# Attention heads taken in pairs in a one-core trunk-layer kernel: unpadded keys, normalised probabilities, transposed output

## The chip, the cores and the metric

One core of one Trainium2 chip runs the kernel. The metric is the device time of one execution in microseconds. The profile is one more execution of the same program.

## The reference, cut to what matters

One trunk layer (adaLN, softmax attention beside a gated linear attention, two branch projections merged by gates, an output projection, a mixture of 32 experts) in float32 for 256 latent and 128 context tokens of width 1024. The part that the change touches:

```python
# 8 query heads, 2 key/value heads, head_dim 64
if latent:
    keys = concat([axial_rope(k_a), ctx_k]); vals = concat([v_a, ctx_v])   # 256 + 128 keys
else:
    keys, vals = k_a, v_a                                                  # 128 keys
sc = einsum('bqkgd,btkd->bkgqt', qblk, kf) * scale
p = softmax(sc, axis=-1)
attn = einsum('bkgqt,btkd->bqkgd', p, vf)
merged = gates[:, :, 0] * (attn @ w_br_attn) + gates[:, :, 1] * (gla @ w_br_gla)
```

## The kernel before, in words

The 384 tokens are three tiles of 128 (0 and 1 latent, 2 context). Engines run programs of their own and meet at semaphores. TensorE's program is written out by hand: it runs 27 projections (`PROJ`, L105; L1478: 8 matmuls of 128x512, each recorded as two MATMULs, as every float32 matmul that is not a transpose), and after projection `j` it works off the list `AFTER[j]` (L108 to L146), which holds small steps of the two attentions. VectorE, ScalarE and GpSimd walk the same lists in the same order (VectorE through `STEPS`, L147). So the small steps of TensorE come between two projections, and VectorE's and ScalarE's part of them runs beside the next projection.

Softmax attention is 24 head jobs (`HEAD_JOBS`, L106: tile 2, then 0, then 1; eight heads each). Two of them go through per step `m`, which lies behind projection `15 + m` (the last three steps, 11 to 13, all lie behind projection 26). In a step TensorE first transposes the probabilities of the two heads of the step before (`pT`, L1615: three 128x128 transposes per latent head, one per context head), then makes the scores of two new heads (`score`, L1608), then multiplies the two heads of two steps before with the values (`pv`, L1626). In the steps 1, 4 and 7 the four transposes of a finished tile of the linear attention (`gT`, L1531) come first.

A score takes all 128 rows: `qT` holds a head of each key/value half in its two row halves (rows 0 to 63 and 64 to 127), and `kTl`, `kTc` hold the keys of each half with zeros in the other 64 rows. VectorE copies them there (L943, two copies per tile) and GpSimd sets the zeros at the start (L620). `score` on VectorE is the negated maximum (L971); ScalarE takes the exponential with its row sum (L1316) into one of four buffers `Pr`. VectorE copies the transposes into `PTr` (L981). `pv` has the transposed probabilities as the stationary operand (128 columns) and 64 columns of the values as the moving one, into `outb[tile]`, tokens in the partitions. When a tile's eight heads are through, VectorE divides by the row sums (`aout`, L986 and L987). Behind all steps TensorE transposes the three tiles (`aT`, L1531), ScalarE copies them to `attnT` (L1332), and the branch projections begin (L1650).

What sets the order around the change: the side jobs (`pT`, `score`, `gT`, `kT`, `z` and others) take three PSUM banks in turn (`Banks`, L150; `side_jobs`, L188), and `claim` waits until the bank's last reader is through. In a step of two `pT` and two `score` jobs the second score has the bank of the first `pT`, which VectorE must have copied out (L981). `gout3` on VectorE (L961 to L964, in the steps 0, 3 and 6) stands behind the step's `score` entry and gives the `gated` that `gT` waits for one step on. The sync queue loads `w_br_attn` and `w_br_gla` (L542) once their weight buffer is free, and `w_out` and the first experts when `aT` of tile 1 is copied (L554).

```python
for _m in range(len(HEAD_JOBS) // 2 + LAG):
    _j = min(15 + _m, len(PROJ) - 1)
    for _n in (2 * _m - 2, 2 * _m - 1): ... ("pT", _n)
    for _n in (2 * _m, 2 * _m + 1): ... ("score", _n)
    for _n in (2 * _m - 4, 2 * _m - 3): ... ("pv", _n), and ("aout", tile) behind head 7
for _j, _i in ((14, 2), (17, 0), (20, 1)):
    AFTER[_j] += [("gout2", _i)]
    AFTER[_j + 1] += [("gout3", _i)]
```

Of the kernel before, what the change touches and what calls it, by code (L numbers as in the profile page):

```python
# [105 lines left out]
HEAD_JOBS = [(i, h) for i in (2, 0, 1) for h in range(HEADS)]  # L106
# [19 lines left out]
LAG = 2  # L126
for _m in range(len(HEAD_JOBS) // 2 + LAG):
# [60 lines left out]
def side_jobs():  # L188
# [15 lines left out]
    jobs += [("aT", i) for i in (2, 0, 1)]  # L204
# [16 lines left out]
def program(nc, T):  # L221
    ctx = ExitStack()
    with ctx:
# [35 lines left out]
        rden = sb("rden", [P, HEADS])  # L259
# [37 lines left out]
        kTl = carve(KV, N_LAT + N_PAST)  # L297
        kTc = carve(KV, N_CTX)
# [36 lines left out]
        def views(gate, up, down0, down1):  # L335
# [81 lines left out]
            "negmax_ready q_ready pv_done gout_exp att_normed gated merged_ready mg_sig ln1_in h2_ready "  # L417
# [22 lines left out]
        for j, w in enumerate(WEIGHTS):  # L440
            _c[j % 2] += 32 if w[0] in ("kvl", "br") else 16
            WCOUNT[w] = _c[j % 2]
# [50 lines left out]
        def _(sp):  # L493
            sp.dma_start(cst[:, :], T["consts"][:, 0:NCONST]).then_inc(S["consts_in"], 16)

            def small_loads():

                sp.wait_ge(S["zeros_set"], 3)
                sp.wait_ge(S["zeros_g"], 7)
# [22 lines left out]
            for j, (kind, n) in enumerate(WEIGHTS):  # L522
# [16 lines left out]
                else:  # L539
                    w = buf.rearrange("p (m k n) -> p m k n", m=2, k=4)  # L540
                    for m, src in enumerate((T["w_br_attn"], T["w_br_gla"])):
                        sp.dma_start(w[:, m], src[0].rearrange("(k p) n -> p k n", p=P)  # L542
                                     [:, :, n * HALF:(n + 1) * HALF]).then_inc(w_in[j % 2], 16)
# [10 lines left out]
            side.wait_read(sp, "aT", 1)  # L554
# [183 lines left out]
        def _(dve):  # L738
# [114 lines left out]
            def block_rows(hh):  # L853
                return slice(hh * DK, (hh + 1) * DK)

            gla_order = {2: 0, 0: 1, 1: 2}
            for kind, a in STEPS:
# [80 lines left out]
                elif kind == "kT":  # L938
                    bank = side.wait_full(dve, "kT", a)
                    for hh in range(2):  # L940
                        dst = kTc[block_rows(hh), hh, :] if a == 2 else \
                            kTl[block_rows(hh), hh, (2 if a == 3 else a) * P:(2 if a == 3 else a) * P + P]
                        ins = V.tensor_copy(dst, bank[block_rows(hh), 0:P])  # L943
                    side.was_read(ins, "kT", a)
# [20 lines left out]
                elif kind == "score":  # L965
# [3 lines left out]
                    if a >= 3:  # L969
                        side.wait_read(dve, "score", a - 3)  # L970
                    V.tensor_reduce(negmax[:, a % 3:a % 3 + 1], bank[:, 0:w], AX.X, ALU.max, negate=True)\  # L971
                        .then_inc(S["negmax_ready"], 1)
                elif kind == "pT":
# [3 lines left out]
                    if a >= 4:  # L977
                        dve.wait_ge(S["pv_done"], a - 3)
# [4 lines left out]
                elif kind == "aout":  # L983
# [897 lines left out]
```

## Time and profile before

| what | value |
|---|---|
| median of 3 runs | 716.77 us (715.06 to 717.89) |
| the profiled execution's own time | 715.41 us |
| its span in the trace | 713.7 us |
| TensorE matmuls busy | 635.1 us, 89% |
| VectorE, ScalarE, GpSimd busy | 39%, 15%, 16% |
| chain that ended last | PE 69%, DMA 15%, DVE 6%, SPq 6% |
| bytes moved | 176.60 MB |

The span is what the trace covers, the time is what the runs are compared by. PE is TensorE's matmuls, PEld its weight loads, DVE is VectorE, ACT is ScalarE, POOL is GpSimd, SPq the sync engine's queue. A busy time of matmuls counts each one's whole duration though they overlap, so what a group of matmuls costs is read from the start of its first to the start of what follows.

### The profile page before, as it was taken

What the parts mean: (1) busy time and instruction counts of PE and PEld (TensorE: products, weight loads), DVE (VectorE), ACT (ScalarE), POOL (GpSimd) and SP (SyncE); (2) the same over time, 40 slices, a digit from 0 to 9 for tenths busy, and PEclk for the clock granted to TensorE, in tenths of its full rate; (3) what the DMA queues carried; (4) which work ended last, traced back from release to release, by engine and by line L of the source; (5) the groups of instructions that cost most, each with busy time, mean ns of one, the idle gap of its engine ahead of it and who ended that gap; (6) DMA issues with size and microseconds to landing.
All of it is one profiled execution on the core that took longest, in us unless ns stands there. A gap on an engine that the chain in (4) does not pass through costs nothing.

```text
span 713.7 us, 8198 instructions
## 1 busy us (share of the span) xinstructions
PE 635.1 (89%) x3225; PEld 346.4 (49%) x3225; DVE 277.9 (39%) x568; ACT 109.6 (15%) x227; POOL 113.1 (16%) x115
## 2 busy tenths in 40 slices
PE   2899999999999999999999974899998888888894
PEld 0374345554444455556444453566664544544431
DVE  2421543236745445213224766133333222322247
ACT  0020252220012122215010020211111001100000
POOL 3000000020300000000000221433333222231100
PEclk9679999999999999999999985799999999999998
DMA  9977444236430230308968087599999999999852
GB/s 337 368 247 252 161 182 149 87 118 236 141 119 5 113 118 1 118 3 298 370 246 321 29 296 292 190 406 405 406 405 405 407 404 403 400 403 402 353 214 88
DMA packets 67495, 176.60 MB, mean 247 GB/s; under 512 B 10420, under 2 KB 12500, under 8 KB 67456
## 3 DMA queue, kind: packets, MB, share of 16 engines
q1 hardware_dynamic: 50832, 143.56, 52.8%
q10 hardware_dynamic: 10880, 24.21, 9.6%
q0 software_dynamic: 5744, 8.28, 3.3%
q8 instruction: 27, 0.44, 0.3%
q14 instruction: 12, 0.10, 0.0%
HBM read 174.55 MB, written 11.96 MB: 261 GB/s over the span
## 4 chain that ended last, share of the span: by engine, by line
PE 69%; DMA 15%; DVE 6%; SPq 6%; issue 2%; ACT 1%; POOL 1%; DVEq 0%; POOLq 0%
PE bank L1478 24%; PE bank L1733 10%; DMA X<-exp_w_up 9%; PE bank L1650 6%; PE bank L1664 6%; PE bank L1742 5%; DMA W<-exp_w_up 3%; DMA X<-w_ada 3%; SPq L451 3%; PE bank L1430 2%; PE bank L1608 2%; PE bank L1626 2%; PE bank L1531 1%; PE bank L1719 1%; SPq L461 1%
## 5 line engine op out<-in xcount | busy, mean ns | idle before, releaser
L1478 PE MATMUL bank<-W,Y 128*128 128x512 f32 (+1 forms) x432 | 183.0, 577 | 0.0
L1478 PEld LDWEIGHTS bank<-W,Y 128*128 128x128 f32 x432 | 80.9, 192 | 85.2 <-issue 82.6
L1733 PE MATMUL bank<-X,Y 128*64 128x256 f32 x704 | 86.6, 401 | 11.0 <-DMA X<-exp_w_up 10.2
L1733 PEld LDWEIGHTS bank<-X,Y 128*64 128x64 f32 x704 | 55.7, 145 | 48.0 <-DMA X<-exp_w_up 19.3
L630 POOL TENSOR_TENSOR rstd<-ss,cst 128x1 f32<-128x1 f32 (+3 forms) x21 | 22.6, 1074 | 339.2 <-DVE ss L760 339.2
L673 POOL DMA_INDIRECT Y<-h_rows,gidx x32 | 41.4, 1293 | 105.4 <-PE bank L1719 93.9
L1139 DVE COPY abias<-bank 128x128 f32<-128x128 f32 x32 | 9.3, 291 | 122.0 <-PE bank L1764 122.0
L1733 PE MATMUL bank<-W,Y 128*64 128x256 f32 (+1 forms) x320 | 39.7, 368 | 9.0 <-DMA W<-exp_w_up 4.6
L1742 PE MATMUL bank<-X,abias 128*64 128x512 f32 x176 | 42.6, 602 | 1.8 <-issue 1.8
L678 POOL DMA_INDIRECT pair_rows<-PTr,sidx x32 | 32.5, 1014 | 65.8 <-DVE PTr L1153 59.3
L1650 PE MATMUL bank<-W,Y 128*128 128x512 f32 x96 | 42.0, 594 | 0.3 <-PE bank L1650 0.3
L1664 PE MATMUL bank<-X,Y 128*128 128x512 f32 x96 | 41.6, 593 | 0.4 <-PE bank L1650 0.4
L1395 ACT ACTIVATE abias<-bank 128x128 f32<-128x128 f32 x32 | 8.9, 278 | 189.4 <-PE bank L1733 189.4
L1733 PEld LDWEIGHTS bank<-W,Y 128*64 128x64 f32 x320 | 25.9, 156 | 21.9 <-DMA W<-exp_w_up 6.8
L981 DVE COPY PTr<-bank 128x384 f32<-128x384 f32 (+1 forms) x24 | 10.1, 464 | 60.9 <-PE bank L1615 60.9
L1153 DVE TENSOR_TENSOR PTr<-bank,abias 128x512 f32<-128x512 f32 x32 | 22.1, 692 | 26.0 <-PE bank L1742 26.0
L1664 PEld LDWEIGHTS bank<-X,Y 128*128 128x128 f32 x96 | 18.1, 190 | 23.2 <-issue 23.2
L1650 PEld LDWEIGHTS bank<-W,Y 128*128 128x128 f32 x96 | 17.9, 190 | 22.3 <-issue 22.3
L821 DVE TENSOR_TENSOR PTr<-bank,abias 128x512 f32<-128x512 f32 x12 | 8.3, 692 | 48.0 <-PE bank L1430 25.5
L1719 PE MATMUL bank<-cst,Y 128*128 128x128 f32 x128 | 21.2, 289 | 5.3 <-DMA Y<-h_rows,gidx 5.3
L1145 DVE SCALAR_TENSOR_TENSOR abias<-PTr,wc,abias 128x512 f32<-128x512 f32 x32 | 24.1, 752 | 1.1
L1258 ACT ACTIVATE X<-bank 128x512 f32<-128x512 f32 (+1 forms) x15 | 8.4, 560 | 99.4 <-PE bank L1478 99.4
(224 smaller groups left out, 705.6 us busy)
## 6 DMA issues: line engine op xcount, KB each, us to landing
X<-exp_w_gate SPq DMA_DIRECT2D x22, 1024.0 KB
X<-exp_w_up SPq DMA_DIRECT2D x22, 1024.0 KB
X<-exp_w_down SPq DMA_DIRECT2D x22, 1024.0 KB, 19.2
W<-w_in SPq DMA_DIRECT2D x8, 2048.0 KB, 9.0
Y<-w_ada ACTq DMA_DIRECT2D x8, 2048.0 KB, 9.2
W<-exp_w_gate SPq DMA_DIRECT2D x10, 1024.0 KB
W<-exp_w_up SPq DMA_DIRECT2D x5, 1024.0 KB
W<-exp_w_down SPq DMA_DIRECT2D x5, 1024.0 KB
```

Of the source, the lines that this page charges most:

```text
L451: eng.dma_start(ebuf[s][0][g].rearrange("p (h c) n -> p h c n", h=2), pick(src, e)).then_inc(landed, 16)
L630: nc.gpsimd.tensor_tensor(rstd[:, 0:n], ss[:, 0:n], const("mhalf", 0, n), ALU.pow)\
L673: pool.indirect_dma_start(G[:, n % NSLOT, :], None, h2_d, bass.IndirectOffsetOnAxis(ap=gidx[:, n:n + 1], axis=0), bounds_check=2 * TOKENS ...
L678: pool.indirect_dma_start(yp_d, bass.IndirectOffsetOnAxis(ap=sidx[:, n:n + 1], axis=0), Yo[:, n % NY, :], None, bounds_check=2 * TOPK * TO ...
L1145: step(V.scalar_tensor_tensor(gw, g2r[:, 1, :], wc[:, n:n + 1], gw, ALU.mult, ALU.add))
L1153: V.tensor_tensor(Yo[:, n % NY, :], banks[6][:, :], gw, ALU.mult).then_inc(S["y_ready"], 1)
L1478: ins = mm(bank[:, 0:cols], hT[:, i, k, :], w[:, k, :], start=k == 0, stop=k == KT - 1)
L1650: ins = mm(bank[:, :], src[:, i, k, :], w[:, m, k, :], start=k == 0, stop=k == 3)
L1664: ins = mm(bank[:, :], mT[:, i, k, :], w[:, k, :], start=k == 0, stop=k == KT - 1)
L1719: ins = tp(banks[0][:, c * P:(c + 1) * P], g[:, :, c], ident)
L1733: ins = mm(bank[hh * 64:hh * 64 + 64, a:b], x_[:, c, h * 64:h * 64 + 64], rhs(hh), start=k == 0 and a == 0, stop=k == KT - 1, skip_group_c ...
L1742: ins = mm(banks[6][o * 64:o * 64 + 64, :], hT_[:, hh * 64:hh * 64 + 64], wd[hh][:, o * HALF:(o + 1) * HALF], start=hh == 0, stop=hh == 1, ...
```

## The change

The heads go in pairs `(j, j + 4)`, one of each key/value half. Both read `qT` and the keys over their own 64 rows, so `kTl` and `kTc` lose their zero halves (one copy per tile, two zeroings fewer). VectorE multiplies the probabilities by the reciprocal of their row sum ahead of the transposes, which wait for that (`p_ready`). `pv` has 64 columns of the values as the stationary operand and the transposed probabilities (128 columns) as the moving one; the two heads of a pair write the rows 0 to 63 and 64 to 127 of `outb[tile]`, which then holds the output transposed. So ScalarE copies it to `attnT` in the step where the tile is through, and `aT` and L986, L987 go. The rows of `w_br_attn` are loaded in the order of the pairs, by two transfers of 64 partitions instead of one of 128.

```diff
-HEAD_JOBS = [(i, h) for i in (2, 0, 1) for h in range(HEADS)]
+HEAD_JOBS = [(i, h) for i in (2, 0, 1) for j in range(HEADS // KV) for h in (j, j + HEADS // KV)]
...
-    for _n in (2 * _m - 4, 2 * _m - 3):
-        if 0 <= _n < len(HEAD_JOBS):
-            AFTER[_j] += [("pv", _n)]
-            if _n % HEADS == HEADS - 1:
-                AFTER[_j] += [("aout", HEAD_JOBS[_n][0])]
+    if 0 <= _m - LAG:
+        AFTER[_j] += [("pv", _m - LAG)]
+        if (_m - LAG) % PAIRED == PAIRED - 1:
+            AFTER[_j] += [("aout", HEAD_JOBS[2 * (_m - LAG)][0])]
...
-    jobs += [("aT", i) for i in (2, 0, 1)]
...
# sync
-                    for m, src in enumerate((T["w_br_attn"], T["w_br_gla"])):
-                        sp.dma_start(w[:, m], ...)
+                    for kv, src in enumerate(T["w_br_attn"][0].rearrange("(a k p) n -> a p k n", a=KV, p=HD)):
+                        sp.dma_start(w[kv * HD:(kv + 1) * HD, 0], src[:, :, cols]).then_inc(w_in[j % 2], 16)
+                    sp.dma_start(w[:, 1], T["w_br_gla"]...)
...
-            side.wait_read(sp, "aT", 1)
+            sp.wait_ge(S["att_ready"], TILES)
# GpSimd
-            for a in (Sl, Sc, kgz, A, kTl, kTc):
+            for a in (Sl, Sc, kgz, A):
# VectorE
-                    for hh in range(2):
-                        dst = kTc[block_rows(hh), hh, :] if a == 2 else ...
-                        ins = V.tensor_copy(dst, bank[block_rows(hh), 0:P])
+                    side.was_read(V.tensor_copy(kTc if a == 2 else kTl[:, at_:at_ + P], bank[:, 0:P]), "kT", a)
...
                     V.tensor_reduce(negmax[:, a % 3:a % 3 + 1], bank[:, 0:w], AX.X, ALU.max, negate=True)
+                    if a % 2 == 1:
+                        for n in (a - 1, a):
+                            hn = HEAD_JOBS[n][1]
+                            side.wait_read(dve, "score", n)
+                            step(V.reciprocal(rden[:, i, hn:hn + 1], rowsum[:, i, hn:hn + 1]))
+                            V.tensor_scalar(Pr[:, n % 4, 0:w], Pr[:, n % 4, 0:w], rden[:, i, hn:hn + 1], None, ALU.mult)
+                                .then_inc(S["p_ready"], 1)
...
-                elif kind == "aout":
-                    step(V.reciprocal(rden[:, :], rowsum[:, a, :]))
-                    tell(V.tensor_tensor(per_head(q[:, a, :], HEADS), per_head(outb[a][:, :], HEADS), ...), "att_normed")
# ScalarE
+                    elif what == "aout":
+                        act.wait_ge(S["pv_done"], PAIRED * ATT_ORDER[a])
+                        A_(attnT[:, a]..., outb[a][:, :], ACT.Copy).then_inc(S["att_ready"], 1)
...
-            for i in (2, 0, 1):
-                bank = side.wait_full(act, "aT", i)
-                side.was_read(A_(attnT[:, i]..., bank[:, :], ACT.Copy), "aT", i)
# TensorE
-                        keys = kTl[:, h // 4, :] if ti < LAT_TILES else kTc[:, h // 4, :]
-                        side.filled(mm(bank[:, 0:keys.shape[1]], qT[:, ti, h % 4, :], keys, start=True, stop=True), ...)
+                        keys = kTl if ti < LAT_TILES else kTc
+                        kv = slice(h // PAIRED * HD, (h // PAIRED + 1) * HD)
+                        side.filled(mm(bank[:, 0:keys.shape[1]], qT[kv, ti, h % PAIRED, :], keys[kv, :], ...), ...)
...
-                        side.wait_read(pe, "score", a)
+                        pe.wait_ge(S["p_ready"], a + 1)
...
-                        for c, v in enumerate(vals):
-                            ins = mm(outb[ti][:, h * HD:(h + 1) * HD], PTr[:, a % 4, c * P:(c + 1) * P], v, ...)
+                        for c, v in enumerate(vals):
+                            for kv in range(KV):
+                                rows = slice(kv * HD, (kv + 1) * HD)
+                                ins = mm(outb[ti][rows, h * P:(h + 1) * P], v[:, rows],
+                                         PTr[:, (2 * a + kv) % 4, c * P:(c + 1) * P], ...)
...
-            for m, i in enumerate((2, 0, 1)):
-                pe.wait_ge(S["att_normed"], m + 1)
-                four(("aT", i), lambda jj: q[:, i, jj * P:(jj + 1) * P])
...
                     if n == 0:
-                        side.wait_read(pe, "aT", i)
+                        pe.wait_ge(S["att_ready"], ATT_ORDER[i])
```

## Rows read from the trace of the kernel before

**Rows 1.** The page: TensorE and DMA busy, tenths in 40 slices of the span.

```profile
PE   2899999999999999999999974899998888888894
...
DMA  9977444236430230308968087599999999999852
```

**Rows 2.** Timeline, step 10, two latent heads: start us, us, engine, line, operation.

```profile
298.56 0.82 PE L1615 MATMUL bank<-cst,X 128*128 128x128 f32 x6
...
299.08 1.02 DVE L981 COPY PTr<-bank 128x384 f32<-128x384 f32 x2 [7.97 <-PE bank L1615]
...
299.21 1.46 PE L1608 MATMUL bank<-X 128*128 128x384 f32 x4
299.70 0.35 PEld L1608 LDWEIGHTS bank<-X 128*128 128x128 f32 x2 [0.29 <-DVE PTr L981]
...
300.50 1.45 PE L1626 MATMUL bank<-X,PTr 128*128 128x64 f32 x12
...
301.79 7.09 PE L1478 MATMUL bank<-W,Y 128*128 128x512 f32 x16
```

**Rows 3.** Chain that ended last (start us, us), an expert's gate and up, 128x128 parts.

```profile
482.56 3.49 PE bank L1733 x64
```

**Rows 4.** Timeline of TensorE, from transposes into matmuls with a stationary operand of 64 columns.

```profile
486.15 0.64 PE L1719 MATMUL bank<-cst,Y 128*128 128x128 f32 x4
486.74 1.94 PE L1742 MATMUL bank<-X,abias 128*64 128x512 f32 x8
```

**Rows 5.** Timeline of TensorE at the end: out of 64 columns, into 64 rows, out.

```profile
687.36 1.94 PE L1742 MATMUL bank<-X,abias 128*64 128x512 f32 x8
689.23 1.13 PE L1774 MATMUL bank<-Y,X 128*128 128x512 f32 x2
690.28 2.85 PE L1779 MATMUL bank<-PTr,X 64*128 64x512 f32 x12
693.06 1.98 PE L1850 MATMUL bank<-X,cst 128*128 128x512 f32 x4
```

**Rows 6.** Timeline of TensorE: scores and values in the steps 2, 4 and 7.

```profile
231.28 0.56 PE L1626 MATMUL bank<-X,PTr 128*128 128x64 f32 x4
231.67 7.09 PE L1478 MATMUL bank<-W,Y 128*128 128x512 f32 x16
...
248.38 1.53 PE L1608 MATMUL bank<-X 128*128 128x384 f32 x4 [0.61 <-ACT Y L1308]
249.74 0.55 PE L1626 MATMUL bank<-X,PTr 128*128 128x64 f32 x4
...
278.30 1.56 PE L1608 MATMUL bank<-X 128*128 128x384 f32 x4
...
279.70 1.45 PE L1626 MATMUL bank<-X,PTr 128*128 128x64 f32 x12
```

**Rows 7.** Timeline, step 0: row sum of its second head, `gout3` on VectorE, then `gT`.

```profile
214.82 0.41 DVE L961 TENSOR_SCALAR X<-X 128x512 f32<-128x512 f32 x1
...
215.40 0.20 ACT L1316 ACTIVATION_READ_ACCUMULATOR X<-bank,negmax 128x1 f32 x1
...
219.37 0.69 DVE L964 TENSOR_TENSOR X<-X 128x512 f32<-128x512 f32 x1
...
221.05 0.60 PE L1531 MATMUL bank<-cst,X 128*128 128x128 f32 x4
```

**Rows 8.** Timeline behind the last projection: last row sum, reciprocal, branch projection, `w_br_attn`'s issue.

```profile
319.15 0.37 SPq L542 DMA_DIRECT2D W<-w_br_attn  x1
...
322.58 0.19 ACT L1316 ACTIVATION_READ_ACCUMULATOR X<-bank,negmax 128x1 f32 x1
...
326.08 0.20 DVE L986 RECIPROCAL rden<-rowsum 128x8 f32<-128x8 f32 x1 [1.93 <-PE bank L1626]
...
327.71 4.53 PE L1650 MATMUL bank<-W,Y 128*128 128x512 f32 x10
```

**Rows 9.** Chain that ended last, at the second pair of key transposes.

```profile
110.76 0.31 DVE X L943
```

More of the change, by code:

```diff
@@ L126 @@
 LAG = 2
+PAIRED = HEADS // KV
+ATT_ORDER = {2: 1, 0: 2, 1: 3}
 for _m in range(len(HEAD_JOBS) // 2 + LAG):
@@ L296, in program @@
         qT = carve(TILES, 4, P)
[L297 to L298 removed]
+        kTl = carve(N_LAT + N_PAST)
+        kTc = carve(N_CTX)
         kc = carve(KV * HD)
@@ L440, in program @@
         for j, w in enumerate(WEIGHTS):
-            _c[j % 2] += 32 if w[0] in ("kvl", "br") else 16
+            _c[j % 2] += {"kvl": 32, "br": 48}.get(w[0], 16)
             WCOUNT[w] = _c[j % 2]
@@ L939, in _ @@
                     bank = side.wait_full(dve, "kT", a)
[L940 to L944 removed]
+                    at_ = (2 if a == 3 else a) * P
+                    side.was_read(V.tensor_copy(kTc if a == 2 else kTl[:, at_:at_ + P], bank[:, 0:P]), "kT", a)
                 elif kind == "gout":
@@ L1329, in _ @@
                             ada_block(a + 1)
-            for i in (2, 0, 1):
-                bank = side.wait_full(act, "aT", i)
-                side.was_read(A_(attnT[:, i].rearrange("p k t -> p (k t)"), bank[:, :], ACT.Copy), "aT", i)
             for i in range(TILES):
@@ L1606, in _ @@
                         bank = side.claim(pe, "score", a)
-                        keys = kTl[:, h // 4, :] if ti < LAT_TILES else kTc[:, h // 4, :]
-                        side.filled(mm(bank[:, 0:keys.shape[1]], qT[:, ti, h % 4, :], keys, start=True, stop=True),
-                                    "score", a)
+                        keys = kTl if ti < LAT_TILES else kTc
+                        kv = slice(h // PAIRED * HD, (h // PAIRED + 1) * HD)
+                        side.filled(mm(bank[:, 0:keys.shape[1]], qT[kv, ti, h % PAIRED, :], keys[kv, :],
+                                       start=True, stop=True), "score", a)
                     elif what == "pT":
                         ti, h = HEAD_JOBS[a]
-                        side.wait_read(pe, "score", a)
+                        pe.wait_ge(S["p_ready"], a + 1)
                         bank = side.claim(pe, "pT", a)
@@ L1617, in _ @@
                     elif what == "pv":
-                        ti, h = HEAD_JOBS[a]
-                        side.wait_read(pe, "pT", a)
+                        ti, h = HEAD_JOBS[2 * a]
+                        for n in (2 * a, 2 * a + 1):
+                            side.wait_read(pe, "pT", n)
                         if h == 0:
-                            pe.wait_ge(S["gla_read"], gla_order[ti])
-                        vcols = slice(KV * HD + (h // 4) * HD, KV * HD + (h // 4 + 1) * HD)
-                        vals = [kvl[:, 0, vcols], kvl[:, 1, vcols], vc[:, (h // 4) * HD:(h // 4 + 1) * HD]] \
-                            if ti < LAT_TILES else [kvl[:, CTX, vcols]]
+                            pe.wait_ge(S["gla_read"], ATT_ORDER[ti])
+                        vals = [kvl[:, 0, KV * HD:], kvl[:, 1, KV * HD:], vc] if ti < LAT_TILES else [kvl[:, CTX, KV * HD:]]
                         for c, v in enumerate(vals):
-                            ins = mm(outb[ti][:, h * HD:(h + 1) * HD], PTr[:, a % 4, c * P:(c + 1) * P], v,
-                                     start=c == 0, stop=c == len(vals) - 1)
+                            for kv in range(KV):
+                                rows = slice(kv * HD, (kv + 1) * HD)
+                                ins = mm(outb[ti][rows, h * P:(h + 1) * P], v[:, rows],
+                                         PTr[:, (2 * a + kv) % 4, c * P:(c + 1) * P],
+                                         start=c == 0, stop=c == len(vals) - 1, skip_group_check=True)
                         ins.then_inc(S["pv_done"], 1)
-            for m, i in enumerate((2, 0, 1)):
-                pe.wait_ge(S["att_normed"], m + 1)
-                four(("aT", i), lambda jj: q[:, i, jj * P:(jj + 1) * P])
             def merged_transposes(i):
```

22 lines of the change are left out of this document (10 added, 12 removed).

## The prediction

> **What bounds the kernel now.** I read the page's slices first. TensorE is busy for nine tenths or more from slice 2 to slice 22, and DMA for nine tenths or more from slice 26 to slice 36 [rows 1]. The changed code lies in the slices 12 to 18, where TensorE is the bound and DMA is mostly free. What TensorE saves there should reach the end whole: the experts' loads of the later slices start on events of the experts' work itself, so the DMA-bound stretch moves forward and does not get longer. Next I read the timeline of a step of two latent heads. It is TensorE's own program: transposes at 298.56, scores at 299.21, values at 300.50, the next projection at 301.79 [rows 2], so 0.65, 1.29 and 1.29 us. VectorE and ScalarE do their part beside the next projection's 7 us.
>
> One thing in that step matters most. The second score's weight load at 299.70 had waited for VectorE's copy of the first head's transposes (1.02 us for two copies from 299.08, so 0.51 us each) [rows 2]. Its matmul can't start before some 299.81, and it takes 384 columns in two recorded matmuls, 1.29 / 2 = 0.64 us. So the scores end at about 300.45 whatever the first one does, and they end at 300.50 now.
>
> **Scores over 64 rows.** That two row halves run side by side shows at the kernel's end: 12 recorded 64-row matmuls of 512 columns take from 690.28 to 693.06, 2.78 us [rows 5]. In a projection 16 recorded ones of 512 columns are 7.09 us busy, the last one's tail included [rows 2], so one lasts 0.427 us, and 12 in a row would be 5.1 us. By that, a latent pair would take 0.64 us instead of 1.29. But the bank wait takes this gain away: I count 0.05 us per latent step. Only in steps 4 and 7, where both scores had waited for ScalarE's copy of `gT`, is there more: 248.38 to 249.74 is 1.36 us and becomes about 0.75, and in step 7 the first score starts at 278.30, and the second, now at 279.70 - 0.64 = 279.06, can start some 0.4 us behind the first, 0.35 us earlier [rows 6]. Context scores are held in the same way by the copy and are bound by their weight loads: nothing.
>
> The Trainium skill's page on TensorEngine Tiling (Array Packing), under Theoretical Speedup, promises up to twice the speed for a contraction of 64; by it the scores would give the 0.64 us in each of 8 latent steps. The trace agrees on the array and differs on what the pair waits for.
>
> **Values stationary.** A pair is now 12 recorded matmuls in 1.29 us (107 ns each, the time of a weight load of 128 columns) and a context pair 4 in 231.28 to 231.67, 0.39 us [rows 2, 6]. Afterwards each has a stationary operand of 64 columns and 128 moving columns, in alternating column halves. The expert stage has that very shape: 64 in 3.49 us, 54.5 ns each [rows 3]. So a latent pair takes 0.65 us (0.64 less) and a context pair 0.22 (0.17 less).
>
> **Changes of the array's shape.** Before, all shapes in a step were 128x128. Now transposes, scores, values and projection have three different ones. Into 64 columns: 486.15 to 486.74 holds four transposes of 0.107 us, which leaves 0.16 [rows 4]. Out of 64 columns: 687.36 to 689.23 less 8 x 0.2135 leaves 0.16; into 64 rows: 689.23 to 690.28 less 2 x 0.427 leaves 0.20; out of 64 rows: 2.78 less 12 x 0.2135 leaves 0.22 [rows 5]. I take 0.18 behind the scores and 0.16 behind the values. The change ahead of the scores falls into the bank wait and costs nothing, except in step 0. Bounds: nothing (the change hides behind the wait for an operand) and 0.3 us.
>
> The Trainium skill's page on TensorEngine Tiling (Array Packing), under Key Properties, says that a change of tiling mode drains TensorE. It gives no figure; the rows above are that drain as this trace has it.
>
> **The steps summed.** Steps 6, 8, 9 and 10: 0.64 + 0.03 - 0.34 = 0.33 each, but I take 0.30 because the wait may hold the second score to the same time: 1.2 us. Step 7: 0.64 + 0.35 - 0.34 = 0.65. Step 4 (values still of context heads): 0.61 + 0.17 - 0.34 = 0.45. Steps 2, 3 and 5: 0.17 - 0.34, so 0.5 us lost in all. Steps 0 and 1 have no values and lose 0.1 and 0.05. Sum: 1.65 us gained.
>
> **Normalising ahead.** Per pair VectorE gets two reciprocals (at most the 0.20 us of the one of 8 columns [rows 8]) and two multiplications (0.41 us for 512 columns in L961 [rows 7], so some 0.33 for 384, 0.18 for 128). They are covered by the projection behind the step. If that cover were gone each step would pay about 1.2 us. But VectorE now waits inside the step for both exponentials, and `gout3` is queued behind: in step 0 it started at 214.82; now it must wait for the row sum at 215.60 and the second reciprocal and multiplication, and starts at about 216.2. Its `gated` moves from 220.06 to about 221.4, and `gT`, which started at 221.05, to about 221.6 [rows 7]. TensorE loses 0.55 us there, with the step's transposes and scores queued behind. For tiles 0 and 1 the same delay just fits into their slack. Bounds: 0 and 3 x 1.4 us.
>
> **The tail.** Steps 11 to 13 have no projection beside them. Now the branch projection starts at 327.71, and the last row sum is there at 322.77 [rows 8]. Afterwards: reciprocal and multiplication to 323.43, the transposes of the last head from 323.6 to 323.93, its copy (behind the other head's, 0.53 us) from 324.1 to 324.65, its values from 324.85 to 325.5, one change of shape, branch projection at 325.66. What goes are the wait for VectorE's division, the exposed `aT` transposes and half of the last values; ScalarE's copy of tile 1 is needed a projection later. 2.05 us gained; between 1.2 (each handoff 0.2 dearer) and 2.8.
>
> **What else moves.** One key copy for two: one of them stood in the chain [rows 9], 0.3 us gained. `w_br_attn` in three issues with `w_br_gla` instead of two: the second set leaves at 319.15 [rows 8], and its projection comes some 20 us later, behind 24 calls of the first half, which hide it; if they didn't, it would be one more issue of 0.37 us per load. ScalarE's `aout` copies run beside projections, as its `aT` copies did not. The two zeroings stand at the start of GpSimd's program behind which first weights are still loading: nothing. `w_out` is asked for about 2 us earlier, into a queue that has just loaded the branch weights: nothing.
>
> **The sum.** 1.65 - 0.55 + 2.05 + 0.3 = 3.45, so 3.5 us less: 711.9 against the profiled execution's 715.41, and 713.3 against the median of 716.77, which stands 1.4 above it. Half a per cent, about what a measurement of this kernel can tell from no change, is 3.6 us. The forecast lies on that line.
>
> **Rivals.**
>
> *The pairs overlap fully.* If the bank wait costs the second score less than I read (the first score is then long through when the second ends), or changes of shape hide, the nominal gains come: 6 x 0.6 us more for the scores. 3.5 + 3.6 = 7.1 us, 709.7. For it: rows 5. Against: the weight load that stands waiting in rows 2.
>
> *VectorE is late.* `gT` waits in all three tiles and the tail's handoffs cost their upper bound: 3.5 - 2 x 0.7 - 0.8 = 1.3 us gained, 715.5. For it: the thin slack of tile 0.
>
> *The tiles don't run side by side.* Then two heads' halves follow each other as before: the values' gain (5 x 0.64 and 4 x 0.17), the 0.96 of steps 4 and 7 and 1.1 of the tail are gone and the changes of shape stay. 3.5 - 3.2 - 0.7 - 1.0 - 1.1 = -2.5, 719.3, and with 0.3 us for each of 22 changes 722. It decides from the point where a values pair takes over 1.0 us. Against it: rows 3 and 5. For it: each moving operand is another one here, as in no row that I read.
>
> **Chances.** Forecast 0.60, full overlap 0.17, VectorE late 0.14, no tiling 0.09. A little under half of the forecast's 0.60 lies beyond 3.6 us, so faster by over 0.5% is 0.29 + 0.17 = 0.46; within 0.5% 0.31 + 0.14 and a small part of the last rival, 0.47; slower the rest of that, 0.07. The range goes from 709.8 to 716.4: it takes in nearly the whole full overlap and the late VectorE and leaves out the last rival.
>
> **What would show it.** Right: a latent step from the transposes' start to the projection's of 2.9 us instead of 3.23; 12 value matmuls in about 0.65; the second score's weight load still waiting for VectorE's copy; `gT` in step 1 waiting for L964; some 6.5 us from the second issue of `w_br_attn` to L1650 instead of 8.56 [rows 8]. Wrong: scores of a latent pair under 1.0 us in an ordinary step; gaps of 0.4 us at the changes of shape; transposes waiting for the multiplication in steps 1 to 11; a later expert stage that doesn't move forward with them.

## The result, and the profile after

The changed kernel took 708.38 us (median of 4 runs, 707.53 to 710.37) where the kernel before took 715.91 in the same comparison (4 runs, 714.52 to 717.89): ratio 0.9903, 95% interval 0.9877 to 0.9928. By that ratio it is 6.9 us less, 5.2 to 8.8 (the two medians lie 7.5 us apart), where 3.5 was forecast (713.3, range 709.8 to 716.4). The sign was right, the forecast gain was half of the measured one, and the median lies below the range.

The page of the changed kernel, TensorE and DMA busy, in tenths of 40 slices:

```profile
PE   2899999999999999999999963999998888888984
DMA  9978445136430230419966196699999999999852
```

The pattern is that of [rows 1], moved forward: first TensorE, then DMA is the bound. The span is 706.8 us against 713.7. From the start of the branch projections to the end of the span both have the same length: 713.7 - 327.71 = 385.99 us and 706.8 - 320.85 = 385.95. So the difference of 6.9 us is there in full when the branch projections begin, and nothing is given back behind them.

A step of two latent heads, from the timeline of the changed kernel. It is the step of [rows 2], which stands behind projection 24 and so is step 9 by the numbering of the lists, not step 10 as its heading says; step 10 takes the same times.

```profile
294.51 0.82 PE L1615 MATMUL bank<-cst,X 128*128 128x128 f32 x6
295.04 1.02 DVE L987 COPY PTr<-bank 128x384 f32<-128x384 f32 x2 [6.12 <-PE bank L1615]
295.26 1.30 PE L1608 MATMUL bank<-X 64*128 64x384 f32 x4
...
295.65 0.29 PEld L1608 LDWEIGHTS bank<-X 64*128 64x128 f32 x2
...
296.49 0.88 PE L1627 MATMUL bank<-PTr,X 128*64 128x128 f32 x12
297.30 7.13 PE L1477 MATMUL bank<-W,Y 128*128 128x512 f32 x16
```

From the transposes to the next projection it is 2.79 us instead of 3.23. The scores take 1.23 us to the start of the values (1.29 before): the row halves save next to nothing here. The values take 0.81 with the change of shape behind them, instead of 1.29. The transposes are followed by the scores after 0.75 us instead of 0.65. The line of 295.65 is the second head's weight load: it comes 0.39 us behind the first score's start, just behind the end of VectorE's first copy of 0.51 to 0.56 us (the two start at 295.04 and take 1.02), so the second score still waits for its bank.

The steps 2, 4 and 7 (as in [rows 6]):

```profile
228.97 0.44 PE L1627 MATMUL bank<-PTr,X 128*64 128x128 f32 x4
229.33 7.13 PE L1477 MATMUL bank<-W,Y 128*128 128x512 f32 x16
...
246.20 0.92 PE L1608 MATMUL bank<-X 64*128 64x384 f32 x4 [0.61 <-ACT Y L1307]
247.05 0.44 PE L1627 MATMUL bank<-PTr,X 128*64 128x128 f32 x4
...
275.35 1.20 PE L1608 MATMUL bank<-X 64*128 64x384 f32 x4
276.49 0.88 PE L1627 MATMUL bank<-PTr,X 128*64 128x128 f32 x12
```

Context values: 0.36 us with the change of shape, 0.39 before. Step 4, where both banks are free when the scores start: 0.85 us instead of 1.36, so the halves do run side by side. Step 7: 1.14 instead of 1.40. So both parts of the forecast show here: 64-row scores overlap where their banks are free, and hardly where the second bank is not.

Step 0, `gout3` on VectorE and the `gT` that waits for it (as in [rows 7]):

```profile
213.35 0.42 DVE L960 TENSOR_SCALAR X<-X 128x512 f32<-128x512 f32 x1
...
217.92 0.69 DVE L963 TENSOR_TENSOR X<-X 128x512 f32<-128x512 f32 x1
...
218.66 0.55 PE L1530 MATMUL bank<-cst,X 128*128 128x128 f32 x3 [0.19 <-DVE X L963]
```

The tail (as in [rows 8]), the last multiplication, the last value products and the branch projection:

```profile
318.28 0.42 DVE L977 TENSOR_SCALAR X<-X,rden 128x384 f32<-128x384 f32 x1
...
319.23 1.69 PE L1627 MATMUL bank<-PTr,X 128*64 128x128 f32 x24
...
320.85 11.43 PE L1649 MATMUL bank<-W,Y 128*128 128x512 f32 x26
```

The wait for the key copy (as in [rows 9]; the `kgT` transposes of tile 0):

```profile
108.32 0.48 DVE L943 COPY X<-bank 128x128 f32<-128x128 f32 x2
...
108.66 0.66 PE L1530 MATMUL bank<-cst,X 128*128 128x128 f32 x4 [0.26 <-DVE X L943]
```

Read from the starts of the projections, the lead of the changed kernel grows like this: 2.12 us at projection 2, the third (projections 0 and 1 run as one group of 32 recorded matmuls; the third starts at 54.27 us before and 52.15 after, and the recorded expectations call it projection 1); still 2.15 just ahead of the key copies; 2.72 at projection 15; 4.88 at projection 26; 6.86 at the branch projections. So the change itself gives 0.57 us at the key copies, 2.16 in the steps 0 to 10 and 1.98 in the tail, 4.7 in all. The other 2.1 us come before projection 2 is under way, where the two programs differ by two zeroings only.

The theory to be tested: the change is worth about 4.7 us, of which the product of the values and its transposed output bring nearly all; the second score is held by VectorE's copy; the rest of the measured 7 us is the chance of when TensorE's clock rises. The rivals: the scores' overlap has a large part, or the start belongs to the change.

### The profile page after: what moved, and what is told of

Its sections match the earlier page's. It is cut to its first block, busy times and chain, and to the rows that moved or that the text cites. A ratio compares the mean times of both kernels' runs of the same rounds, so it can differ in the third digit from the quotient of the medians.

```text
span 706.8 us, 8217 instructions
## 1 busy us (share of the span) xinstructions
PE 628.4 (89%) x3213; PEld 334.1 (47%) x3213; DVE 285.2 (40%) x606; ACT 108.8 (15%) x227; POOL 111.9 (16%) x113
## 4 chain that ended last, share of the span: by engine, by line
PE 67%; DMA 17%; DVE 7%; SPq 4%; issue 2%; ACT 1%; POOL 1%; ACTq 0%; DVEq 0%; POOLq 0%
PE bank L1477 23%; PE bank L1732 10%; DMA X<-exp_w_up 8%; DMA Y<-exp_w_up 6%; PE bank L1649 6%; PE bank L1663 6%; PE bank L1741 4%; PE bank L1429 3%; SPq L451 2%; DMA W<-w_ada 2%; PE bank L1608 2%; PE bank L1530 1%; SPq L465 1%; PE bank L1718 1%; PE bank L1627 1%
## 5 line engine op out<-in xcount | busy, mean ns | idle before, releaser
L987 DVE COPY PTr<-bank 128x384 f32<-128x384 f32 (+1 forms) x24 | 10.2, 464 | 46.0 <-PE bank L1615 45.9
```

## The experiments

In all of them "the stretch" is the time from the start of projection 2 to the start of the branch projections: 327.71 - 54.27 = 273.44 us in the trace of before, 320.85 - 52.15 = 268.70 in that of the changed kernel. It leaves out both ends, whose length differs between profiles of one kernel. Ratios are to the kernel before, run beside each group of experiments on the same chip (25, 19 and 18 runs of it, medians 715.05, 714.86 and 714.73 us, on three different chips).

### The changed kernel again

Edit: none.

> The changed kernel once more, for two things. First the size: the two traces differ by 4.7 us from the key copies on (0.57 there, 2.16 in the attention steps, 1.98 in the tail) and by 2.15 us before projection 0 is through, in code that the change leaves alone but for two zeroings. If those 2.15 us are the chance of one execution (when TensorE's granted clock goes up), the kernel is 4 to 6 us faster than the one before in ten runs, and projection 0's start (42.44 us in the first trace, 43.49 before) and that of projection 3 scatter by 2 us from profile to profile. If they belong to the change, the gain is 6.5 to 8 us and projection 0 starts at 42.4 again. Second: a latent step takes 2.79 us again, from the first transpose to the next projection.

Measured: 709.15 us, ratio 0.9928 (0.9904 to 0.9952), so 5.1 us less (3.4 to 6.9). The stretch is 322.46 - 53.78 = 268.68 us, as in the first trace to 0.02. Projections 0 and 1 (one line) and projection 2 in the timeline of this run:

```profile
43.30 8.70 PE L1477 MATMUL bank<-W,Y 128*128 128x288 f32 x32
53.78 4.15 PE L1477 MATMUL bank<-W,Y 128*128 128x288 f32 x16
```

and in the first profile of the changed kernel:

```profile
42.44 7.93 PE L1477 MATMUL bank<-W,Y 128*128 128x288 f32 x32
52.15 4.15 PE L1477 MATMUL bank<-W,Y 128*128 128x288 f32 x16
```

The same program is 1.63 us apart at projection 2. What was expected from chance came: a gain of 4 to 6 us and a start that moves. Behind the stretch it moves as well: from the branch projections to the end of the span this profile has 384.24 us and the first one 385.95. Step 9 and its projection take 9.75 us again (9.76 in the first trace).

### Scores over 128 rows again

```diff
-                        keys = kTl if ti < LAT_TILES else kTc
...
-                        side.filled(mm(bank[...], qT[kv, ti, h % PAIRED, :], keys[kv, :], ...)
+                        keys = kTl[:, h // PAIRED, :] if ti < LAT_TILES else kTc[:, h // PAIRED, :]
+                        side.filled(mm(bank[...], qT[:, ti, h % PAIRED, :], keys, ...)
```

with the padded `kTl`, `kTc`, their zeroings and their two copies.

> The changed kernel with the scores over 128 rows again, keys padded with zeros (and two key copies and the two zeroings, as before). If the second score is held by VectorE's copy of the first transposes, this costs next to nothing in an ordinary latent step (scores 1.29 us instead of 1.23 and one change of shape fewer, 0.0 to 0.1 us), some 0.6 us in step 4, 0.35 in step 7 and 0.57 at the key copies: 1 to 2 us slower than the changed kernel. If the two row halves do overlap, each of eight latent steps gets 0.4 to 0.6 us longer: 4 to 5 us slower than the changed kernel.

Measured: 710.52 us (8 runs), ratio 0.9945 (0.9926 to 0.9964). The stretch is 321.87 - 51.47 = 270.40 us, 1.7 more than the changed kernel's. A latent step in its timeline (step 9):

```profile
295.52 0.82 PE L1617 MATMUL bank<-cst,X 128*128 128x128 f32 x6
296.18 1.46 PE L1610 MATMUL bank<-X 128*128 128x384 f32 x4
297.56 0.88 PE L1629 MATMUL bank<-PTr,X 128*64 128x128 f32 x12
298.37 7.13 PE L1480 MATMUL bank<-W,Y 128*128 128x512 f32 x16
```

2.85 us against 2.79. So 64 rows are worth 0.06 us in an ordinary latent step. Nearly all of the 1.7 us lies where it was expected: 0.57 at the key copies, 0.61 in step 4 and 0.35 in step 7; another 0.12 is in step 0. The first theory's 1 to 2 us came, not the rival's 4 to 5. This kernel has the zeroings, and in this profile its projection 2 starts at 51.47 us, earlier than in any profile of the changed kernel: they don't hold up the start.

### The values moving again

```diff
-                                ins = mm(outb[ti][rows, h * P:(h + 1) * P], v[:, rows],
-                                         PTr[:, (2 * a + kv) % 4, c * P:(c + 1) * P], ...)
+                                ins = mm(outb[ti][:, hq * HD:(hq + 1) * HD], PTr[:, (2 * a + kv) % 4, c * P:(c + 1) * P],
+                                         v[:, kv * HD:(kv + 1) * HD], ...)
...
+                elif kind == "aout":
+                    tell(V.tensor_copy(q[:, a, :], outb[a][:, :]), "att_normed")
...
+            for m, i in enumerate((2, 0, 1)):
+                pe.wait_ge(S["att_normed"], m + 1)
+                four(("aT", i), lambda jj: q[:, i, jj * P:(jj + 1) * P])
```

and the rows of `w_br_attn` loaded by one transfer again, as before.

> The changed kernel with the product of the values turned back: probabilities stationary, values moving, output by tokens, copied by VectorE and transposed at the end. By the sum of the prediction the values of a latent pair take 1.29 us again instead of 0.65, less one change of shape of 0.16 us: 0.48 us in five steps, nothing for context heads, and in the tail the last values, VectorE's copy and the transposes, some 2 us or more: 4.5 to 5.5 us slower than the changed kernel. If the gain of the change lay in the scores or in the start of the kernel, this is 1 to 2 us slower only.

Measured: 715.05 us (12 runs), ratio 0.9999 (0.9981 to 1.0017). The stretch is 328.58 - 54.11 = 274.47 us, 5.8 more than the changed kernel's, a little over what was expected. Without this part the whole change brings nothing. Of the 5.8 us, 2.7 lie in the tail and 3.1 in the steps 2 to 10. The tail's part shows in the tail of this kernel's timeline:

```profile
321.49 1.55 PE L1631 MATMUL bank<-X,PTr 128*128 128x64 f32 x12
323.18 1.11 PE L1619 MATMUL bank<-cst,X 128*128 128x128 f32 x6
324.13 2.79 PE L1631 MATMUL bank<-X,PTr 128*128 128x64 f32 x24
326.75 1.60 PE L1534 MATMUL bank<-cst,X 128*128 128x128 f32 x12
328.58 1.96 PE L1656 MATMUL bank<-W,Y 128*128 128x512 f32 x4 [0.23 <-issue]
```

The last values take 2.62 us (the changed kernel 1.62), and then come 1.83 us of output transposes: 9.09 us from the transposes of step 11 at 319.49 to the branch projection, against 6.35 (314.50 to 320.85) in the changed kernel. An ordinary latent step takes 3.37 us (298.38 to 301.75) against 2.79; in the kernel before it was 3.23.

### The normalisation ahead, alone

The edits of the last two together. What is left of the change is the pair order and

```diff
+                            step(V.reciprocal(rden[:, i, hn:hn + 1], rowsum[:, i, hn:hn + 1]))
+                            V.tensor_scalar(Pr[:, n % 4, 0:w], Pr[:, n % 4, 0:w], rden[:, i, hn:hn + 1], None, ALU.mult)
...
-                    tell(V.tensor_tensor(per_head(q[:, a, :], HEADS), per_head(outb[a][:, :], HEADS), ...), "att_normed")
+                    tell(V.tensor_copy(q[:, a, :], outb[a][:, :]), "att_normed")
```

> The kernel before with the pair order and the normalisation ahead of the transposes alone; scores over 128 rows, values moving, VectorE copies the output instead of dividing it. Expected against the kernel before: gT of tile 2 waits up to 0.5 us longer, the tail gets the last reciprocal and multiplication (0.6 us) in front of the last transposes, and a copy stands where reciprocal and division stood (0.2 us less): 0.5 to 1 us slower, 716.5 against 715.9. If the zeroings or the order of the pairs had a part in the gain at the start, this is not slower, or faster.

Measured: 715.03 us (12 runs), ratio 1.0005 (0.9987 to 1.0024). The stretch is 326.67 - 52.32 = 274.35 us, 0.9 more than before, inside what was expected; in the runs it doesn't show. So normalising ahead costs up to a microsecond by itself. It is needed because the row sums belong to tokens, and the division by them must be done while tokens are in the partitions; that allows the transposed output.

These four kernels make a square. With the values moving, 64-row scores and the single key copy are worth nothing (274.47 us with them, 274.35 without); with the values stationary they are worth 1.7 us (268.70 against 270.40). With the values moving they gain 0.57 us at the key copies, 0.13 in step 0, 0.42 in step 4 and 0.16 in step 7 and lose 0.13 to 0.29 in each of the steps 2, 3, 5, 6, 8, 9 and 10, where they bring the only changes of the array's shape. So "the values bring nearly all" was too simple: stationary values alone take 3.95 us off (274.35 to 270.40), and the scores' 1.7 us come on top only with them.

### Values ahead of scores

```diff
+    _first = 0 <= _m - LAG and _m < len(HEAD_JOBS) // 2 - 1
+    if _first:
+        AFTER[_j] += [("pv", _m - LAG)]
     for _n in (2 * _m, 2 * _m + 1):
         if _n < len(HEAD_JOBS):
             AFTER[_j] += [("score", _n)]
     if 0 <= _m - LAG:
-        AFTER[_j] += [("pv", _m - LAG)]
+        if not _first:
+            AFTER[_j] += [("pv", _m - LAG)]
```

> The changed kernel with the values product of a step ahead of its scores (steps 2 to 10; the tail keeps its order). The second score then finds its bank copied out. If VectorE's copy of the first transposes is what holds the second score in an ordinary step, the scores of a latent pair now take 0.64 us plus a change of shape instead of 1.23, and a latent step goes from 2.79 to about 2.5 us in steps 6 and 8 to 10, 0.25 us each; step 5 gains the same, steps 4 and 7 little or nothing, since their scores wait for ScalarE's copy of gT anyway: 1.2 to 1.8 us faster than the changed kernel between projection 1 and the branch projection. If row halves don't overlap in this kernel, scores still take 1.28 us behind the values and nothing is gained.

Measured: 705.98 us (6 runs), ratio 0.9881 (0.9852 to 0.9909). A latent step of its timeline (step 9):

```profile
293.38 0.82 PE L1619 MATMUL bank<-cst,X 128*128 128x128 f32 x6
294.13 0.88 PE L1631 MATMUL bank<-PTr,X 128*64 128x128 f32 x12
294.94 0.30 PEld L1612 LDWEIGHTS bank<-X 64*128 64x128 f32 x4 [0.17 <-issue]
294.94 0.92 PE L1612 MATMUL bank<-X 64*128 64x384 f32 x4
295.78 4.56 PE L1481 MATMUL bank<-W,Y 128*128 128x512 f32 x10
```

The same instructions in another order: scores in 0.84 us instead of 1.23, the step 2.40 instead of 2.79. All four weight loads now run through in 0.30 us from 294.94, where the second head's came 0.39 us behind the first in the changed kernel. VectorE's two copies were through by then (293.91 to 294.93). The array changes its shape three times in either order and transposes and values take 0.75 and 0.81 us in both, so the 0.39 us are the wait for the second score's bank. From projection 15 to 26 the kernel takes 305.15 - 203.64 = 101.51 us against 104.06 in the changed kernel, 2.5 us less, more than the expected 1.2 to 1.8: the ordinary steps gained 0.39 instead of 0.25 each, and the steps 2, 3 and 4 gained 0.31, 0.37 and 0.33 that were not expected, while step 7 lost 0.45.

In the stretch it saves only 1.5 us (318.94 - 51.75 = 267.19). The missing microsecond is in the windows from 165 to 175 us. Behind the stretch's length stand the busy times of TensorE, its weight loads, VectorE, ScalarE and GpSimd; the first number behind them is the granted clock, as a share of 2.4 GHz, and then come DMA's share and GB/s. This kernel:

```profile
165.00:175.00 10.00, 8.82 (x29) 3.95 (x26) 7.84 (x21) 0.00 (x0) 1.64 (x1) 0.83 0.71 261
```

and the changed kernel in its first profile:

```profile
165.00:175.00 10.00, 8.82 (x52) 4.00 (x46) 7.47 (x21) 0.39 (x1) 1.64 (x1) 1.00 0.74 276
```

In this execution the clock fell for a part of that window, right behind a place where TensorE had waited 1.2 us for VectorE: the projection that starts at 167.07 takes 8.83 us, where the same one takes 7.13 in the kernel with both orders and added matmuls (below), behind the same wait. That happened in 2 of 14 profiles.

### Matmuls nobody reads, at the start

```diff
+            def filler(n):
+                for _ in range(n):
+                    mm(banks[6][:, :], ident, cst[:, 0:HALF], start=True, stop=True, skip_group_check=True)
             pe.wait_ge(S["consts_in"], 16)
+            filler(3)
...
                 if n:
                     columns(colbank, 8 * (n - 1), n - 1)
+                filler((5, 2, 2, 0)[n])
```

> The changed kernel with 12 matmuls whose result nobody reads, put where TensorE waits for the first weights. Four profiles of kernels with the same start have projection 0 at 39.35, 41.01, 42.44 and 43.3 to 43.6 us, and the granted clock is at its lower level (1.2 GHz) from 20 us on until it rises at some time between 28 and 45 us. If that rise is the whole scatter, the clock is at 2.4 GHz throughout here, projection 0 starts at about 39 us, and the runs lie closer together and 1.5 to 3 us lower than the changed kernel's. If the scatter comes from the transfers, the added matmuls change nothing or cost up to 3 us.

Measured: 709.16 us (8 runs, 707.24 to 710.88), ratio 0.9924 (0.9898 to 0.995). A miss: no faster than the changed kernel, and no closer together. Projection 2 started at 51.79 us and projection 0 at 42.08, not 39; the granted clock was 0.64 of 2.4 GHz from 20 to 25 us and 0.68 from 25 to 30, so the added matmuls didn't keep it up. They also stood in the way: four of the recorded ones took from 24.80 to 28.37 us, at 1.2 GHz, and the matmuls that the kernel needed next began behind them at 28.37 (26.15 and 25.82 in the first and third profile of the changed kernel). The clock's part in the start is neither shown nor refuted by this run.

### The same, and before the experts

```diff
+                if i == TILES - 1:
+                    filler(3)
                 second_transposes(i)
...
+            filler(6)
             pe.wait_ge(S["both_ready"], 1)
...
+            filler(1)
             index_tables(0)
+            filler(4)
             next_tokens(0)
```

> The same, and 14 more such matmuls where TensorE waits for the second normalisation, the router's choice and the first rows of the experts. There the granted clock falls to 1.2 GHz after 4.2 us without a matmul and stays so until 447 us; the first expert's gate and up take 5.19 us instead of 3.45. At 2.4 GHz the router's matmuls (3.63 us now, 1.96 before the fall), the index tables and the first expert would be 3 to 5 us faster, and since the experts' loads start on them, the end moves forward by as much: 4 to 7 us below the changed kernel. If the stretch is bound by VectorE and the transfers alone, it is as e6.

Measured: 703.62 us (6 runs), ratio 0.986 (0.9829 to 0.9891), 5.5 us below the changed kernel, and as much below the kernel with the matmuls at the start only, which ran beside it (709.16). In the profiles of those two the stretch is 0.1 us apart (268.80 and 268.69) and the time from the branch projections to the end 5.45 (385.21 and 379.76), so the gain lies there. Windows of this stretch where the router and the first expert stand, changed kernel (second profile):

```profile
415.00:450.00 35.00, 17.84 (x90) 14.81 (x90) 14.62 (x55) 5.01 (x8) 10.26 (x10) 0.56 0.68 259
```

For the kernel with both orders and these matmuls (below) it is:

```profile
415.00:450.00 35.00, 29.52 (x167) 18.52 (x169) 14.72 (x58) 6.40 (x11) 10.47 (x11) 0.95 0.79 293
```

In this kernel's own profile the granted clock is 0.95 there too. With it the serial chain of the router runs through sooner, and the loads that follow it move with it: the first expert's gate and up take 3.67 us instead of 6.33 in the kernel with the matmuls at the start only. Six of the added matmuls are more than the wait holds: VectorE had the router's choice ready at 426.0 us and TensorE was done with them at 427.2, so by these two times fewer of them might gain about another microsecond (an estimate; that was not run).

### The kernel before with the same matmuls

Edit: the last two diffs on the kernel before.

> The kernel before with the same 26 added matmuls as in e7. It measures the change again with the clock's chance taken out: e7 should be below this by the 4.75 us that the traces show between the second projection and the branch projections (4.3 to 5.2), where the timed pairs so far gave 7.0 and 5.1. If some of the gain came from elsewhere, the difference is 6 us or more.

Measured: 711.3 us (12 runs, 707.02 to 714.08), ratio 0.9947 (0.9924 to 0.997). The kernel of the last experiment is 7.7 us below it in the medians, more than the 4.75 expected; in the means it is 6.9, with an interval of about 2 us to either side. The expectation had said that 6 us or more would mean a gain from elsewhere, so this run speaks for one, within its scatter. Its stretch is 326.21 - 51.81 = 274.40 us, 5.7 more than the 268.69 of the last experiment; about 1 us of it is again a fallen clock at 165 to 175 us. The two profiles are 6.7 us apart: 0.4 at the start, 5.7 in the stretch and 0.6 behind it. What is left over the stretch's 4.7 and that fallen clock I can't name. Its runs scatter by 7 us, so the clock's chance was not taken out as I had meant.

### The best of them

Edit: values ahead of scores and all the added matmuls, on the changed kernel.

> The order of e5 (values ahead of scores) and the added matmuls of e7 together, as the version that should beat both kernels. e5's attention steps were 2.5 us shorter than the changed kernel's, e7 5.5 us below it in its runs. The two lie in different stretches, so if the gains add up: 709.1 - 2.5 - 5.5, so 700 to 703 us, and 266.2 us from projection 1 to the branch projections where TensorE's clock doesn't fall at 165 to 175 us. If e5's runs had profited from the clock only, 703.5 as e7.

Measured: 700.97 us (6 runs, 698.62 to 701.47), ratio 0.9799 (0.9771 to 0.9827): 14.4 us below the kernel before by the ratio and 8 to 9 below the changed one (709.15 and 709.80). The stretch is 319.29 - 53.14 = 266.15 us, as expected. The two gains add up.

### The kernel before again, the zeroings, and the changed kernel a third time

> The kernel before, once more, for a second profile of it. By theory, its 273.44 us from the start of projection 1 to the branch projections come again, to 0.1 us, or 274.4 where the granted clock falls at 165 to 175 us as in e5 and e8; the changed kernel had 268.70 and 268.68. If it is 274.4 or more without such a fall, the first trace of before was a lucky one and the gain of the change in that stretch is larger than 4.75 us. Runs against runs of the same kernel: ratio 1.000 within its interval.

> The changed kernel with the two zeroings of GpSimd given back (0.95 us of work at the start, VectorE's first operation stretched by them). Two of three kernels with the zeroings started projection 1 at 51.5 to 52.3 us and one at 54.3, and those without at 51.8 to 54.1, so they should not matter: same time as e12 within a third of a per cent. If the part of the gain that the traces don't show hangs on them, 1 to 2 us slower than e12.

```diff
-            for a in (Sl, Sc, kgz, A):
+            for a in (Sl, Sc, kgz, A, kTl2, kTc2):
```

`kTl2` and `kTc2` are arrays of twice the width, whose first halves are the keys.

> The changed kernel a third time, beside e10 and e11 on the same chip. 268.7 us from projection 1 to the branch projections, and a ratio to the kernel before of 0.992 to 0.9935 (4.75 to 5.7 us). A ratio of 0.990 or less would mean that the traces miss a part of the gain.

Measured: before again, 714.4 us (12 runs), ratio 0.9997 (0.9975 to 1.0018), stretch 329.23 - 55.81 = 273.42 us. The zeroings, 708.95 us (6 runs), ratio 0.9919 (0.9892 to 0.9945), stretch 320.78 - 52.09 = 268.69. Changed kernel, 709.8 us (7 runs), ratio 0.9932 (0.9905 to 0.996), stretch 321.53 - 52.85 = 268.68. In the stretch the kernels repeat to 0.02 us, and they differ by 4.74 us. The zeroings do nothing. Projections 0 and 1 (one line) and projection 2 of the second profile of before:

```profile
44.81 9.22 PE L1478 MATMUL bank<-W,Y 128*128 128x288 f32 x32
55.81 4.15 PE L1478 MATMUL bank<-W,Y 128*128 128x288 f32 x16
```

Windows from 20 to 60 us (granted clock behind the busy times): the first profile of before, the changed kernel's first, and the kernel with padded scores, one line each.

```profile
20.00:60.00 40.00, 37.47 (x171) 23.16 (x172) 12.34 (x29) 5.64 (x15) 1.11 (x2) 0.72 0.87 290
```

```profile
20.00:60.00 40.00, 37.81 (x176) 21.71 (x177) 12.83 (x29) 5.63 (x15) 1.10 (x2) 0.76 0.89 308
```

```profile
20.00:60.00 40.00, 34.47 (x178) 19.65 (x179) 12.84 (x29) 5.53 (x15) 1.10 (x2) 0.89 0.92 310
```

The order of the clocks (0.72, 0.76, 0.89) is that of the starts of projection 2 (54.27, 52.15, 51.47 us). Over all 14 profiles it holds roughly: the five with 0.72 to 0.77 start projection 2 at 52.15 to 55.81 us, the nine with 0.86 to 0.91 at 51.45 to 53.14. It is a sign and no proof, and the clock is not alone: in the changed kernel's third profile the clock is full from 20 to 30 us, but TensorE then waits 0.34 and 2.51 us for loads of `w_ada`, for which it doesn't wait in the first, at 1.2 GHz.

## Why the prediction was wrong

By its own steps, in the traces:

| step of the sum | forecast | measured |
|---|---|---|
| ordinary latent step (6, 8, 9, 10) | 0.30 each | 0.34, 0.40, 0.40, 0.39 |
| step 7 | 0.65 | 0.69 |
| step 4 | 0.45 | 0.49 |
| steps 2, 3, 5 together | -0.5 | -0.34 |
| steps 0 and 1, with `gT`'s wait | -0.15 - 0.55 | +0.12 - 0.33 |
| tail | 2.05 | 1.98 |
| key copies | 0.3 | 0.57 |
| sum | 3.45 | 4.71 |

**The bank wait was right.** The second score waits for VectorE's copy, so 64 rows give 0.06 us in an ordinary step; the step with values ahead of scores shows it (scores 0.84 instead of 1.23 us). The Trainium skill's factor of two under Theoretical Speedup, on its page on TensorEngine Tiling (Array Packing), holds for the array only: it comes out of step 4 (0.85 us instead of 1.36, a change of shape of some 0.18 included) and of the reordered kernel, not of an ordinary step of the change as it was made. The rival of full overlap is refuted, though its 709.7 us was nearest to the measured time; that it came so near is luck.

**The values were right.** Turning them back costs all that the change had brought, though that includes the scores' 1.7 us, which come only beside them. 12 recorded matmuls and one change of shape take 0.81 us, the 0.65 and 0.16 of the forecast. The drain at a change of tiling mode, which the Trainium skill's page on TensorEngine Tiling (Array Packing) names under Key Properties, is small here, as rows 4 and 5 had it. The rival without tiling is refuted by that row. The rival that VectorE is late is refuted as well: `gT` waits 0.19 us for it, once. The tail came as forecast: 6.54 us from the second issue of `w_br_attn` (314.31) to the branch projection, where some 6.5 was named.

**Terms that were mis-sized.** All but the tail (0.07 us less than forecast) lie on the same side. Context scores were put at nothing, and with their change of shape at a small loss; where both their banks are free (steps 0 and 1) they take 0.43 us with it instead of 0.55 (210.91 to 211.34; before, 213.63 to 214.18). `gout3` was delayed as forecast (it starts 213.35 - 211.34 = 2.01 us behind its projection's start instead of 0.64, so 1.37 later), but `gT` follows it after 0.05 us where I had allowed 0.2. The key copies were taken at one shorter copy in the chain; TensorE's wait (0.56 us in the old trace, 0.26 now) and what stood behind it gave 0.57. And the ordinary steps gained 0.04 to 0.10 us more. Together that is 1.3 us (4.71 instead of 3.45). In the sum itself a latent pair of scores stood once with 0.05 us and once with 0.03, which changes nothing.

**The step that failed** is the last one, from the sum to the measured time. "711.9 against the profiled execution's 715.41, and 713.3 against the median of 716.77" treats the ends of the kernel as fixed. They are not: projection 2 starts between 51.5 and 55.8 us in profiles of nearly the same program, the part behind the stretch takes 384.2 to 386.0 us without matmuls added there, and the runs of one kernel scatter with a standard deviation of 1.3 us (changed) and 1.7 us (before), so that two groups of 4 runs differ by some 2 us by chance. The range had no term for it, and its base, the median of 3 runs, was itself high: the kernel before has a mean of 714.9 us over the 66 runs beside the comparisons, 1.8 below the 716.77.

The 4.9 us from the forecast 713.3 to the measured 708.4 add up like this: 0.9 is the median of before, which was 715.91 in the comparison and not 716.77; 1.3 are the mis-sized terms; 2.8 are left, and no step of the sum is about them. In the two first profiles 2.1 us of lead stand ahead of projection 2, where a second profile of the changed kernel is 1.6 us later and a second one of before 1.5.

Not all of that is chance. The changed kernel's 17 runs have a mean of 709.2 us, 5.7 below the 714.9 of before, with an interval of about 5.0 to 6.4; the 4.7 us of the stretch lie just under it. So about a microsecond of the gain stands outside the stretch, more than the runs' scatter easily gives, and its cause stays open. Both profiles of the kernel before have a late projection 2 (54.27 and 55.81 us), and none of the experiments shows why; the zeroings are not it.

## What to carry to other kernels

Two matmuls on different rows of the array overlap only if both can start: before counting on it, look at whether the second one's weight load stands waiting for a PSUM bank, and put work that needs no bank between. Turning a product round, so that the narrow operand is stationary and the output comes out transposed, paid twice here: by half the array time and by the transposes and copies that went from the path. Weigh such parts together: 64-row scores gave nothing while the values moved and 1.7 us beside stationary ones. And a gain under one per cent is read from a stretch of the trace that repeats, such as from one projection to another; the whole time carries what the clock did in the waits.

## What the runs showed that was not expected

- A stretch of 268.7 us repeats to 0.02 us from execution to execution (to 0.1 with matmuls added at the start), while the whole kernel's runs range over 3 to 7 us. The scatter sits where TensorE waits: at 15 to 45 us, at 165 to 175 (granted clock 0.83 over these 10 us in two profiles and 1.00 in twelve, behind a wait of 1.2 us) and around the router (0.52 to 0.63 of 2.4 GHz from 415 to 450 us without added matmuls).
- Matmuls that nobody reads, put into the waits around the router, made the kernel 5.5 us faster (703.62 against 709.16), with the granted clock at 0.95 there. At the start of the kernel they brought nothing.
- The changes of shape of the array cost 0.1 to 0.2 us each and can hide behind a wait.
